# Moving the modulation's partial sums out of two feed-forward up projections

## The chip, the cores and the metric

One core of one Trainium2 chip runs the whole program. The metric is the device time of that core in microseconds (us); lower is better. Engines are named as the profile names them: PE is TensorE (PEld its weight loads), DVE is VectorE, ACT is ScalarE, POOL is GpSimd, SP is SyncE, which here only issues DMAs.

## What is computed

A small transformer stack on one sequence of 256 tokens of width 1024, to which 16 meta tokens are prepended (L = 272) for the first two layers. All of it is float32.

```python
h = concat([meta, x])
h = h + fox_attention(h)              # w_in: 4096 columns (q, k, v, gate) and 16 forget logits
h = h + conv_ffn(h)                   # down(silu(conv3(x @ gate)) * (x @ up)), hidden width 2816
h = h + hgrn2_mixer(h)                # w_in: f, q, g, v
h = h + conv_ffn(h)
h = h[:, 16:]
mod = (silu(c) @ w_ada + b_ada).reshape(3, 3, 1024)    # 9216 numbers
def sublayer(h, i, fn, w):
    shift, scale, gate = mod[i]
    u = rms_norm(h) * (1 + scale) + shift
    return h + w * gate * rms_norm(fn(u))
h = sublayer(h, 0, swiglu)            # "glu1"
h = sublayer(h, 1, token_mixer)       # "mix_in", two attentions, "branch", "mix_out"
h = sublayer(h, 2, swiglu)            # "glu2"
```

The change is about `mod`. It depends on nothing but `c`, `w_ada` and `b_ada`, so it can be worked out at any time before the three sublayers that use it.

## The kernel before

**The stream of weights.** Each projection is cut into units: 256 output columns with all 1024 input rows (1 MB), or 128 output columns with 2816 input rows for the down projections (1.4 MB). Two units, s = 0 and s = 1, make a pair, and a pair is one iteration of a hardware loop. SP loads a unit into `raw[s]`. The float32 product is made of three products of rounded values, so ACT rounds the unit to `w_hi[s]` (line 421, once PE has finished the unit that was in that slot), DVE subtracts to get `w_lo[s]` (L958), and PE multiplies hi by hi, hi by lo and lo by hi (L1899). When PE has done a unit, DVE (or ACT) evacuates its PSUM banks. In `ffn0_up` and `ffn1_up` that evacuation is long: a scale (L1344), six operations of the 3-tap convolution (L1348, L1353), another scale (L1359), a product (L1363) and a subtraction (L1365).

**The chains.** `w_ada` is cut into 36 pairs of 256 columns. For each pair POOL loads two halves of 512 KB into `ada_raw[0]` and `ada_raw[1]` (L1820, `load_modulation`); it issues each half when DVE has finished with what was there. DVE forms a running sum with 8 operations in a row, 4 for each half (`ada_half`: L969 for the first, L978 for the others; below, "a chain"). PE then adds up the 128 partitions with two matmuls of one column against ones (`ada_sums`, L1870), which land in bank 5 of PSUM. The chains are spread over the projections: inside `gemm`, after the split of each unit, DVE works on half a chain. The table `ADA` says which iterations carry one: name: (first pair, first iteration, number of iterations). `sums` in the PE program says after which iterations PE adds a pair up, one iteration after DVE has made it:

```python
                pe.wait_ge(ada_mult, p * 2 + 4)
                for s in range(2):
                    T_.matmul(ps[:, 5, bass.ds(p * 2 + s, 1)], ada_sum[:, s * P:(s + 1) * P], ones[:, 0:1],
                              start=True, stop=True).then_inc(ada_done, 1)
```

PE executes in order, so a wait for `ada_mult` (a finished chain) holds up the matmuls that stand behind it.

**Order.** Everything is ordered by hand: each engine has its own program, and semaphores tie them (`hi_ready`, `lo_ready`, `unit_done`, `banks_free`). The finished columns of `mod` are read from PSUM by `read_modulation`, from places named by `before_last` (between the last two iterations of a loop), and before bank 5 is needed for something else: `near_scores` waits for `mod_read`. Between the first and the second segment of `hgrn_in` (f, then q), DVE computes `f_all` from the gates with eight operations (L1388) and `kk` with one (L1390). POOL, when it has issued its ninth pair, clears `near` and `s_t` for the HGRN mixer with two MEMSETs (L1835, L1836).

Of the kernel before, what the change touches and what calls it, by code (L numbers as in the profile page):

```python
# [27 lines left out]
P = 128  # L28
# [96 lines left out]
def build_program(nc, t):  # L125
# [43 lines left out]
    ADA = {"fox_out": (0, 0, 1), "ffn0_up": (1, 4, 3), "ffn0_down": (4, 0, 3), "hgrn_in": (7, 0, 2), "hgrn_out": (9, 0, 1),  # L169
           "ffn1_up": (10, 5, 2), "ffn1_down": (12, 0, 3), "glu1_up": (15, 0, 11), "glu1_down": (26, 0, 2), "mix_in": (28, 0, 4), "glu2_up": (32, 0, 4)}  # L170
# [5 lines left out]
    with ctx:  # L176
# [230 lines left out]
        def _(act):  # L407
# [174 lines left out]
            nc.scalar.activation(c_silu, vecs("c_2", 0, KD), ACT.Sigmoid).then_inc(c_gate, 1)  # L582
# [363 lines left out]
        def _(dve):  # L946
# [37 lines left out]
            def gemm(name, evac=None, k=None, per=0, late=False, defer=False, ada=None, before_last=None):  # L984
                g = GEMMS[name]
                first, ada_it, ada_pairs = ADA[ada] if ada else (0, 0, 0)
                for i, (at, s) in enumerate(g["segs"]):
# [4 lines left out]
                    peel = before_last is not None or last and (defer or at + 2 * pairs >= N_UNITS or UNIT_SIZE[at + 2 * pairs] != g["size"])  # L992
# [178 lines left out]
            gemm("fox_in", copy_out(lambda it, s: proj1[:, bass.ds(it * 4 + 2 * s, 2), :], L), k=0)  # L1171
# [25 lines left out]
            dve.wait_ge(vec_ready, 4)  # L1197
            for i in range(2):
# [113 lines left out]
            dve.wait_ge(c_ready, 1)  # L1312
# [15 lines left out]
            def h_and_squares(it, s, pair):  # L1328

                h_of_down(it, s, pair)  # L1330
                if s > 0 and not (s == 2 and type(it) is int and it == KD // 2 - 1):
                    add_square("ffn1_down", it, s - 1)

            def conv_ffn(l):
# [35 lines left out]
                gemm(f"ffn{l}_up", evac, per=2, late=True, ada=f"ffn{l}_up", before_last=modulation_post0 if l else None)  # L1370
# [13 lines left out]
            gemm("hgrn_in", out_from(0), k=0, late=True, ada="hgrn_in")  # L1384
# [6 lines left out]
            def modulation_0():  # L1391
                read_modulation(1, 0, 18)
                pre_gain(0)
                dve.wait_ge(mod_set, 1)
                V.memset(lam_tmp[:, 0:1], 0.0).then_inc(mod_ready, 1)

            gemm("hgrn_in", out_from(8), k=1, before_last=modulation_0)
# [119 lines left out]
            def gained_tile(i, name):  # L1517

                def evac(it, s, pair):
                    if s < 2:  # L1520
# [3 lines left out]
                        V.tensor_scalar(y_raw[:, k, :], ps[:, 2 * s:2 * s + 1, 0:SEQ], mod_g[:, i, k], None, ALU.mult).then_inc(banks_free[s], 1)  # L1524
                    if s > 0 and not (s == 2 and type(it) is int and it == KD // 2 - 1):
# [64 lines left out]
            def modulation_1():  # L1590
                read_modulation(3, 24, 56)
                pre_gain(1)
                post_gain(1)
                dve.wait_ge(mod_set, 4)
                V.memset(lam_tmp[:, 0:1], 0.0).then_inc(mod_ready, 1)

            def modulation_2():
# [6 lines left out]
                dve.wait_ge(mod_set, 5)  # L1604
                V.memset(lam_tmp[:, 0:1], 0.0).then_inc(mod_ready, 1)

            def modulation_3():
                read_modulation(5, 64, 72)
                post_gain(2)
                dve.wait_ge(mod_set, 6)  # L1610

            def glu1():
# [13 lines left out]
                gemm("glu1_down", gained_tile(0, "glu1_down"), defer=True, ada="glu1_down", before_last=modulation_1)  # L1626
# [35 lines left out]
            gemm("mix_in", copy_out(lambda it, s: proj2[:, bass.ds(it * 4 + 2 * s, 2), :], SEQ), k=0, ada="mix_in", before_last=modulation_2)  # L1662
# [799 lines left out]
```

## Time and profile before

| | |
|---|---|
| median of 3 runs | 1517.8 us (1512.83 to 1521.1) |
| the profiled execution | 1515.93 us, its span 1514.3 us |
| PE busy | 1410.7 us, 93% of the span |
| DVE busy | 993.5 us, 66% |
| ACT busy | 600.9 us, 40% |
| POOL busy | 81.4 us, 5% |
| mean granted TensorE clock | 0.970 |

The span is the time from the first to the last instruction; the execution's own time is 1.6 us more. A busy share is an average over stages; the rows below are read by stage.

### The profile page before, as it was taken

Reading aid. Unit: us, or ns where it says so; the run is one execution under the profiler, and the core shown is the slowest. Engines: PE = TensorE matmul, PEld = TensorE weight load, DVE = VectorE, ACT = ScalarE, POOL = GpSimd, SP = SyncE. Lnnn points to the kernel's source line nnn. Section 1 sums busy time; section 2 is a strip of 40 time slices with the busy share of each in tenths; the row PEclk is TensorE's granted clock in tenths of the full one; section 3 lists DMA queues with packets and bytes.
Section 4 is the critical chain, followed back from the end, with each engine's and each line's share of the span. In section 5 each row is a group of like instructions: output and inputs, shape, how many; then the busy total and the mean of one; then the engine's idle time right before and its main releaser. Section 6 shows DMA issues by size and latency. Waiting matters only on the chain.

```text
span 1514.3 us, 29508 instructions
## 1 busy us (share of the span) xinstructions
PE 1410.7 (93%) x11888; PEld 1362.1 (90%) x11888; DVE 993.5 (66%) x1288; ACT 600.9 (40%) x590; POOL 81.4 (5%) x108
## 2 busy tenths in 40 slices
PE   5989898998999989899899899999899988899997
PEld 4988788998999989799899899999798878899997
DVE  4474455688765785568886687875685345796654
ACT  2344123443424424444343444343333454544432
POOL 2020000000000100000000011100020000000000
PEclk9999888999999999999999999999899999999998
DMA  5443204456775543345677577896373333475672
GB/s 167 139 116 107 84 1 140 153 182 218 201 219 179 165 132 101 127 163 185 204 203 218 163 250 259 271 267 201 111 259 125 112 123 107 146 243 187 187 191 66
DMA packets 263069, 252.53 MB, mean 167 GB/s; under 512 B 4681, under 2 KB 250572, under 8 KB 262996
## 3 DMA queue, kind: packets, MB, share of 16 engines
q1 hardware_dynamic: 251808, 212.37, 45.7%
q0 software_dynamic: 10992, 39.06, 7.6%
q8 instruction: 55, 0.90, 0.2%
q14 instruction: 18, 0.15, 0.0%
q10 hardware_dynamic: 196, 0.06, 0.0%
HBM read 250.42 MB, written 1.05 MB: 166 GB/s over the span
## 4 chain that ended last, share of the span: by engine, by line
PE 76%; DVE 11%; ACT 6%; issue 5%; DMA 1%; DVEq 0%; ACTq 0%; SPq 0%
PE ps L1899 62%; ACT w_hi L421 4%; DVE w_lo L958 3%; PE ps L1975 2%; PE ps L1923 2%; DVE proj L978 1%; PE ps L2124 1%; DMA raw<-in_fox_w_in 1%; PE ps L2059 1%; PE ps L2341 1%; PE ps L2109 1%; PE ps L2103 1%; DMA raw<-in_ffn_w_down 1%; DVE proj L1353 0%; PE ps L2020 0%
## 5 line engine op out<-in xcount | busy, mean ns | idle before, releaser
L1899 PE MATMUL ps<-x_hi,w_hi 128*128 128x272 f32 (+2 forms) x2208 | 642.3, 291 | 26.1 <-DVE w_lo L958 12.1
L1899 PE MATMUL ps<-x_lo,w_hi 128*128 128x272 f32 (+2 forms) x2208 | 633.2, 287 | 0.0
L1899 PE MATMUL ps<-x_hi,w_lo 128*128 128x272 f32 (+2 forms) x2208 | 632.9, 287 | 0.0
L958 DVE TENSOR_TENSOR w_lo<-raw,w_hi 128x2048 fp32r<-128x2048 f32 (+1 forms) x185 | 451.2, 2439 | 190.5 <-ACT w_hi L421 190.1
L421 ACT ACTIVATE w_hi<-raw 128x2048 fp32r<-128x2048 f32 (+1 forms) x185 | 374.3, 2023 | 409.4 <-PE ps L1899 376.3
L1899 PEld LDWEIGHTS ps<-x_hi,w_hi 128*128 128x128 f32 x2208 | 421.4, 191 | 33.4 <-issue 27.5
L1899 PEld LDWEIGHTS ps<-x_lo,w_hi 128*128 128x128 f32 x2208 | 421.7, 191 | 0.3
L1899 PEld LDWEIGHTS ps<-x_hi,w_lo 128*128 128x128 f32 x2208 | 421.8, 191 | 0.0
L1899 PE MATMUL ps<-g_hi,w_hi 128*128 128x256 f32 (+2 forms) x768 | 219.2, 285 | 8.6 <-DVE w_lo L958 3.3
L1899 PE MATMUL ps<-g_hi,w_lo 128*128 128x256 f32 (+2 forms) x768 | 217.8, 284 | 0.0
L1899 PE MATMUL ps<-g_lo,w_hi 128*128 128x256 f32 (+2 forms) x768 | 217.2, 283 | 0.0
L1899 PEld LDWEIGHTS ps<-g_hi,w_hi 128*128 128x128 f32 x768 | 145.4, 189 | 10.5 <-issue 3.5
L1899 PEld LDWEIGHTS ps<-g_lo,w_hi 128*128 128x128 f32 x768 | 145.8, 190 | 0.0
L1899 PEld LDWEIGHTS ps<-g_hi,w_lo 128*128 128x128 f32 x768 | 145.3, 189 | 0.0
L978 DVE SCALAR_TENSOR_TENSOR proj<-v_tok,small,proj 128x256 f32<-128x256 f32 x252 | 122.2, 485 | 7.7
L1820 POOL DMA_DIRECT2D v_tok<-in_w_ada x72 | 54.0, 751 | 1155.9 <-DVE proj L978 816.6
L1899 PE MATMUL ps<-proj_r,w_hi 128*128 128x258 f32 (+1 forms) x256 | 49.6, 296 | 7.8 <-DVE proj_r L1710 5.3
L1899 PEld LDWEIGHTS ps<-proj_r,w_hi 128*128 128x128 f32 x256 | 41.8, 199 | 8.8 <-issue 5.7
L481 ACT ACTIVATE proj<-ps 128x256 f32 (+2 forms) x20 | 8.5, 427 | 97.0 <-PE ps L1899 97.0
L1353 DVE SCALAR_TENSOR_TENSOR proj<-proj,cols 128x272 f32<-128x272 f32 (+1 forms) x88 | 39.6, 491 | 6.3 <-DVE proj L1348 3.4
L630 ACT ACTIVATE g_hi<-proj 128x544 f32 (+3 forms) x22 | 14.2, 648 | 70.5 <-DVE proj L1363 70.5
L1038 DVE COPY proj<-ps 128x544 f32 (+2 forms) x24 | 16.9, 702 | 36.2 <-PE ps L1899 31.5
(315 smaller groups left out, 1323.2 us busy)
## 6 DMA issues: line engine op xcount, KB each, us to landing
raw<-in_ffn_w_gate SPq DMA_DIRECT2D x44, 1024.0 KB, 5.3
raw<-in_ffn_w_up SPq DMA_DIRECT2D x44, 1024.0 KB, 5.3
raw<-in_ffn_w_down SPq DMA_DIRECT2D x32, 1408.0 KB, 7.0
v_tok<-in_w_ada POOLq DMA_DIRECT2D x72, 512.0 KB, 4.4
raw<-in_w_in SPq DMA_DIRECT2D x20, 1024.0 KB, 5.3
raw<-in_fox_w_in SPq DMA_DIRECT2D x16, 1024.0 KB, 5.8
raw<-in_hgrn_w_in SPq DMA_DIRECT2D x16, 1024.0 KB, 5.4
raw<-in_fox_w_out SPq DMA_DIRECT2D x4, 1024.0 KB, 4.8
```

What stands on the lines that cost most here:

```text
L421: nc.scalar.activation(w_hi[s][:, 0:size], raw[s][:, 0:size], ACT.Copy).then_inc(hi_ready, 1)
L958: V.tensor_tensor(w_lo[s][:, 0:size], raw[s][:, 0:size], w_hi[s][:, 0:size].bitcast(F32), ALU.subtract).then_inc(lo_ready, 1)
L978: ins = V.scalar_tensor_tensor(out=ada_sum if whole else ada_acc, in0=ada_raw[s][:, k, :], scalar=c_k, in1=ada_acc, op0=ALU.mult, op1=ALU.add)
L1038: V.tensor_copy(dst(it, s), ps[:, 2 * s:2 * s + 2, 0:T]).then_inc(banks_free[s], 1)
L1353: ins = V.scalar_tensor_tensor(out=conv[:, m, 0:T], in0=pad_a[:, m, w:w + T], scalar=col(w, it, m), in1=conv[:, m, 0:T], op0=ALU.mult, op1 ...
L1820: pool.dma_start(ada_raw[s], ada_w[:, KD // 2 * s:KD // 2 * (s + 1), bass.ds((it + first) * (2 * P), 2 * P)]).then_inc(ada_landed[s], 16)
L1899: ins = T_.matmul(dst, w[:, kt, m * P:(m + 1) * P], x[:, kt, 0:T], start=(kt == 0 and i == 0), stop=(kt == kts - 1 and i == 2))
L1923: ins = T_.matmul(ps[:, 2 * s + m, 0:T], wt[:, kt, m * P:(m + 1) * P], x[:, kt, 0:T], start=(kt == 0 and i == 0), stop=(kt == KD - 1 and i ...
L1975: ins = T_.matmul(ps[:, 4, 0:T], ones, sq[:, k, 0:T], start=(k == 0), stop=(k == KD - 1))
L2059: ins = T_.matmul(ps[:, b + 2 * e + bank, at:at + nk], proj1_flat[r, j * L + qt * P:j * L + (qt + 1) * P], proj1[r, 8 + j, 0:nk], start=Fa ...
L2103: T_.matmul(dst, c_diag[:, key0:key0 + P], shift_r[:, t0:L], start=(kt == 0), stop=False, skip_group_check=True)
L2109: ins = T_.matmul(ps[:, 2 * p + e, at:at + n], proj1_flat[r, (8 + j) * L + kt * P:(8 + j) * L + (kt + 1) * P], proj1[r, j, t0:L], start=Fa ...
```

## The change

The 36 chains are dealt out anew. `ffn0_up` loses 3 and `ffn1_up` loses 2. The first segment of `fox_in` gets 2, the q segment of `hgrn_in` gets 1 (`hgrn_q`), `glu1_down` goes from 2 to 3 and `mix_in` from 4 to 5. Nothing changes in how many there are, nor in what one consists of. With that go:

- The sums stand in columns 288 and up of bank 5 (`ADA_COL`), beside the forget logits, and the first four are copied out at once.
- silu(c) is made at the start: Exp on ACT, then an addition, a reciprocal and a product on DVE, instead of Sigmoid on ACT and a product on POOL.
- In the down projections PE adds a pair up after the first unit of the iteration instead of after the second (`sums_after=0`).
- `modulation_0`, `modulation_1` and `modulation_2` and the post gain of sublayer 0 are read inside the evacuation of a last iteration, instead of between two iterations; for this the last iteration is written out (`unroll_last`).
- POOL issues pairs 0 and 1 during `fox_in`, before it builds `c_diag`.

```diff
-    ADA = {"fox_out": (0, 0, 1), "ffn0_up": (1, 4, 3), "ffn0_down": (4, 0, 3), "hgrn_in": (7, 0, 2), "hgrn_out": (9, 0, 1),
-           "ffn1_up": (10, 5, 2), "ffn1_down": (12, 0, 3), "glu1_up": (15, 0, 11), "glu1_down": (26, 0, 2), "mix_in": (28, 0, 4), "glu2_up": (32, 0, 4)}
+    ADA = {"fox_in": (0, 1, 2), "fox_out": (2, 0, 1), "ffn0_down": (3, 0, 3), "hgrn_f": (6, 0, 2), "hgrn_q": (8, 0, 1), "hgrn_out": (9, 0, 1),
+           "ffn1_down": (10, 0, 3), "glu1_up": (13, 0, 11), "glu1_down": (24, 0, 3), "mix_in": (27, 0, 5), "glu2_up": (32, 0, 4)}
+    ADA_COL = 288
...
+            act.wait_ge(vec_ready, 1)
+            nc.scalar.activation(c_silu, vecs("c_2", 0, KD), ACT.Exp, scale=-1.0).then_inc(c_gate, 1)
...
-            nc.scalar.activation(c_silu, vecs("c_2", 0, KD), ACT.Sigmoid).then_inc(c_gate, 1)
...
             def modulation_post0():
-                read_modulation(2, 18, 24)
+                read_modulation(3, 18, 26)
...
-            gemm("fox_in", copy_out(lambda it, s: proj1[:, bass.ds(it * 4 + 2 * s, 2), :], L), k=0)
+            dve.wait_ge(c_gate, 1)
+            steps.done(V.tensor_scalar(c_silu, c_silu, 1.0, None, ALU.add))
+            steps.wait()
+            steps.done(V.reciprocal(c_silu, c_silu))
+            steps.wait()
+            V.tensor_tensor(c_silu, c_silu, vecs("c_2", 0, KD), ALU.mult).then_inc(c_ready, 1)
+            dve.wait_ge(c_ready, 1)
+            gemm("fox_in", copy_out(lambda it, s: proj1[:, bass.ds(it * 4 + 2 * s, 2), :], L), k=0, ada="fox_in")
+            dve.wait_ge(ada_done, 4 + 2)
+            V.tensor_copy(mod[:, 0:4], ps[:, 5, ADA_COL:ADA_COL + 4]).then_inc(mod_read, 1)
...
+                if type(it) is int and it == KD // 2 - 1 and s == 0:
+                    modulation_post0()
...
-                gemm(f"ffn{l}_up", evac, per=2, late=True, ada=f"ffn{l}_up", before_last=modulation_post0 if l else None)
+                gemm(f"ffn{l}_up", evac, per=2, late=True)
...
-            gemm("hgrn_in", out_from(8), k=1, before_last=modulation_0)
+            gemm("hgrn_in", q_out, k=1, ada="hgrn_q", unroll_last=True)
...
+            pool.wait_ge(unit_done, 2 + 1)
+            load_modulation(0, 2)
...
-            load_modulation(0, ADA["hgrn_out"][0])
+            load_modulation(2, ADA["hgrn_out"][0] - 2)
...
-                        if add:
-                            ada_sums(it + ada_before)
+                            if add and s == sums_after:
+                                ada_sums(it + ada_before)
...
-            gemm("ffn0_up", from_norm(1), xh, xl, L, late=lambda: norm_sum(1, L), ada="ffn0_up", sums=(5, 8))
-            gemm("ffn0_down", from_hidden(0), gh, gl, L, ada="ffn0_down", sums=(1, 4))
+            gemm("ffn0_up", from_norm(1), xh, xl, L, late=lambda: norm_sum(1, L))
+            gemm("ffn0_down", from_hidden(0), gh, gl, L, ada="ffn0_down", sums=(1, 4), sums_after=0)
...
-            gemm("hgrn_in", from_norm(2), xh, xl, L, k=1, ada="hgrn_out", sums=(0, 1))
+            gemm("hgrn_in", from_norm(2), xh, xl, L, k=1, ada="hgrn_q", sums=(0, 2))
...
-            gemm("ffn1_down", from_hidden(1), gh, gl, L - UNUSED, ada="ffn1_down", sums=(1, 4))
+            gemm("ffn1_down", from_hidden(1), gh, gl, L - UNUSED, ada="ffn1_down", sums=(1, 4), sums_after=0)
```

Three places in the order of instructions. The names: `w_lo<-raw,w_hi` is the split of a unit; `proj<-v_tok,small,proj` and `proj<-v_tok,small` are operations of a chain (`ada_raw` lies in `v_tok`); `proj<-ps,rstd` is an evacuation. Lines of the changed kernel are its own, a few more than those of the kernel before.

DVE, the loop of the iterations of `ffn0_up` that carry a chain, before:

```order
L958 TENSOR_TENSOR w_lo<-raw,w_hi 128x2048
L964 ISA
L965 ISA
L969 TENSOR_SCALAR proj<-v_tok,small 128x256
L122 ISA
L978 SCALAR_TENSOR_TENSOR proj<-v_tok,small,proj 128x256
...
L1348 TENSOR_SCALAR proj<-proj,cols 128x272
```

and in the changed kernel, the one loop that is left:

```order
L960 TENSOR_TENSOR w_lo<-raw,w_hi 128x2048
L1360 REGISTER_ALU
L1362 ISA
L1362 REGISTER_ALU
L1362 TENSOR_SCALAR proj<-proj,cols 128x272
```

The half chain between the split and the convolution is gone, and so is the other half behind the second split.

DVE, from the end of the f segment of `hgrn_in` into the q segment, before:

```order
L1390 TENSOR_SCALAR proj<-scratch 128x2176
L1013 UNCONDITIONAL_BRANCH
L1150 TENSOR_TENSOR proj<-ps,rstd 128x544
L958 TENSOR_TENSOR w_lo<-raw,w_hi 128x2048
L1150 TENSOR_TENSOR proj<-ps,rstd 128x544
L958 TENSOR_TENSOR w_lo<-raw,w_hi 128x2048
L1013 REGISTER_ALU
```

and now:

```order
L1404 TENSOR_SCALAR proj<-scratch 128x2176
L1015 UNCONDITIONAL_BRANCH
L1152 TENSOR_TENSOR proj<-ps,rstd 128x544
L960 TENSOR_TENSOR w_lo<-raw,w_hi 128x2048
L971 TENSOR_SCALAR proj<-v_tok,small 128x256
L980 SCALAR_TENSOR_TENSOR proj<-v_tok,small,proj 128x256 x3
L1152 TENSOR_TENSOR proj<-ps,rstd 128x544
L960 TENSOR_TENSOR w_lo<-raw,w_hi 128x2048
L980 SCALAR_TENSOR_TENSOR proj<-v_tok,small,proj 128x256 x4
L1015 REGISTER_ALU
```

The q segment's first iteration has a chain now; the eight operations of `f_all` and the one of `kk` ahead of it stand where they stood.

PE, the sum in the loop of `ffn1_down`, before (the last matmuls of the second unit, the sum, the branch back):

```order
L1899 MATMUL ps<-g_hi,w_lo 128x258
L1868 ISA
L1870 ISA
L1870 MATMUL ps<-const_f_sb,proj 128x1
L1870 ISA
L1870 MATMUL ps<-const_f_sb,proj 128x1
L1954 REGISTER_ALU
L1954 COMPARE_AND_BRANCH
```

and now (the last matmul of the first unit, the sum, the first matmul of the second unit):

```order
L1926 MATMUL ps<-g_hi,w_lo 128x258
L1895 ISA
L1897 ISA
L1897 MATMUL ps<-const_f_sb,proj 128x1
L1897 ISA
L1897 MATMUL ps<-const_f_sb,proj 128x1
L1915 REGISTER_ALU
L1926 MATMUL ps<-g_hi,w_hi 128x258
```

The sum stands one unit earlier on PE; the chain that it waits for stands where it stood on DVE.

## Rows read from the trace of the kernel before

**Rows 1.** The page: busy us (share of the span) xinstructions.

```profile
PE 1410.7 (93%) x11888; PEld 1362.1 (90%) x11888; DVE 993.5 (66%) x1288; ACT 600.9 (40%) x590; POOL 81.4 (5%) x108
```

**Rows 2.** Windows, ffn0_up: us, busy PE PEld DVE ACT POOL, clock, DMA, GB/s.

```profile
283.40:319.70 36.30, 36.30 (x290) 36.30 (x289) 28.93 (x37) 15.12 (x12) 0.00 (x0) 1.00 0.53 173
334.70:349.70 15.00, 13.02 (x102) 12.75 (x102) 13.18 (x20) 5.06 (x6) 1.52 (x3) 1.00 0.62 210
```

**Rows 3.** PE's waits, 320:400 (ffn0_up) and 717:786.3 (ffn1_up): total, times, longest.

```profile
PE ps L1899 <- DVE w_lo L958: 5.1, 5, 1.1
...
PE ps L1899 <- DVE w_lo L958: 4.2, 4, 1.4
```

**Rows 4.** The chain that ended last (start, us, what): a sum on PE.

```profile
1133.93 0.34 PE ps L1870 x4
```

**Rows 5.** Timeline of PE in ffn1_down: start, us, what, [idle before <-releaser].

```profile
819.94 0.36 PE L1899 MATMUL ps<-g_hi,w_hi 128*128 128x258 f32 x1 [0.28 <-DVE w_lo L958]
...
828.12 0.39 PE L1899 MATMUL ps<-g_hi,w_hi 128*128 128x258 f32 x1
...
836.15 0.50 PE L1870 MATMUL ps<-const_f_sb,proj 128*128 128x1 f32 x4
```

**Rows 6.** Timeline of DVE, ffn1_down: first and third of three second half chains.

```profile
810.66 2.04 DVE L978 SCALAR_TENSOR_TENSOR proj<-v_tok,small,proj 128x256 f32<-128x256 f32 x4
...
845.28 2.04 DVE L978 SCALAR_TENSOR_TENSOR proj<-v_tok,small,proj 128x256 f32<-128x256 f32 x4
```

**Rows 7.** Timelines, glu1_down: a second half chain on DVE, ACT behind the next unit.

```profile
1015.55 2.04 DVE L978 SCALAR_TENSOR_TENSOR proj<-v_tok,small,proj 128x256 f32<-128x256 f32 x4
1017.89 0.39 ACT L481 ACTIVATE proj<-ps 128x256 f32 x1 [5.38 <-PE ps L1899]
```

**Rows 8.** Timeline of DVE, ffn0_down: the evacuation behind a second half chain.

```profile
431.45 0.44 DVE L1067 TENSOR_TENSOR h<-h,ps 128x272 f32 x1 [0.78 <-PE ps L1899]
```

**Rows 9.** Timelines of DVE and PE, fox_in's first segment and its end.

```profile
60.45 0.73 DVE L1038 COPY proj<-ps 128x544 f32 x1 [1.93 <-PE ps L1899]
...
90.09 0.57 PE L1899 MATMUL ps<-x_hi,w_hi 128*128 128x272 f32 x1 [5.37 <-DVE scratch L1176]
```

**Rows 10.** Timeline of POOL, around the MEMSETs for the HGRN mixer.

```profile
497.99 0.75 POOL L1820 DMA_DIRECT2D v_tok<-in_w_ada  x1 [8.02 <-DVE proj L978]
498.73 0.65 POOL L1835 MEMSET scratch<- 128x640 f32 x1
499.30 3.01 POOL L1836 MEMSET scratch<- 128x3456 f32 x1
```

**Rows 11.** Timeline of DVE (last row PE): a first operation in ffn0_up, then hgrn_in.

```profile
323.88 0.34 DVE L969 TENSOR_SCALAR proj<-v_tok,small 128x256 f32<-128x256 f32 x1
...
495.31 2.04 DVE L978 SCALAR_TENSOR_TENSOR proj<-v_tok,small,proj 128x256 f32<-128x256 f32 x4
...
501.36 1.09 DVE L969 TENSOR_SCALAR proj<-v_tok,small 128x256 f32<-128x256 f32 x1
...
507.42 2.04 DVE L978 SCALAR_TENSOR_TENSOR proj<-v_tok,small,proj 128x256 f32<-128x256 f32 x4
509.37 2.73 DVE L1388 TENSOR_SCALAR scratch<-proj,small 128x272 f32<-128x272 f32 x8
512.14 1.30 DVE L1390 TENSOR_SCALAR proj<-scratch 128x2176 f32<-128x2176 f32 x1
...
517.70 2.29 DVE L958 TENSOR_TENSOR w_lo<-raw,w_hi 128x2048 fp32r<-128x2048 f32 x1 [0.80 <-ACT w_hi L421]
516.32 0.39 PE L1899 MATMUL ps<-x_hi,w_hi 128*128 128x272 f32 x1 [0.27 <-DVE w_lo L958]
```

**Rows 12.** An idle stretch of PE, and two windows (clock: third from last).

```profile
259.81 0.36 PE L1899 MATMUL ps<-x_hi,w_hi 128*128 128x272 f32 x1 [1.73 <-DVE x_lo L1135]
260.40:263.30 2.90, 2.90 (x14) 2.90 (x14) 2.02 (x6) 2.90 (x4) 0.00 (x0) 0.50 0.06 20
...
736.80:742.60 5.80, 5.80 (x48) 5.65 (x48) 5.42 (x11) 0.75 (x2) 0.75 (x1) 1.00 0.79 270
```

More of the change, by code:

```diff
@@ L982, in ada_half, with gemm @@
                 ins.then_inc(ada_mult, 1)
-            def gemm(name, evac=None, k=None, per=0, late=False, defer=False, ada=None, before_last=None):
+            def gemm(name, evac=None, k=None, per=0, late=False, defer=False, ada=None, before_last=None, unroll_last=False):
                 g = GEMMS[name]
@@ L991, in gemm @@
                     last = at + 2 * pairs == g["first"] + g["units"]
-                    peel = before_last is not None or last and (defer or at + 2 * pairs >= N_UNITS or UNIT_SIZE[at + 2 * pairs] != g["size"])
+                    peel = unroll_last or before_last is not None or last and (defer or at + 2 * pairs >= N_UNITS or UNIT_SIZE[at + 2 * pairs] != g["size"])
                     def body(it, size, ahead=False, defer=False, ada=False):
@@ L1382, in out_from @@
                 return normed_out(lambda it, s: proj1[:, bass.ds(it * 4 + (tile0 + 2 * s), 2), :])
-            gemm("hgrn_in", out_from(0), k=0, late=True, ada="hgrn_in")
+            gemm("hgrn_in", out_from(0), k=0, late=True, ada="hgrn_f")
             dve.wait_ge(gates_done, 4)
@@ L1390, in _, with q_out @@
             V.tensor_scalar(kk, f_all, -1.0, 1.0, ALU.mult, ALU.add).then_inc(f_ready, 1)
[L1391 to L1395, printed above, removed]
-            gemm("hgrn_in", out_from(8), k=1, before_last=modulation_0)
+            q_normed = out_from(8)
+            def q_out(it, s, pair):
+                q_normed(it, s, pair)
+                if type(it) is int and it == 1 and s == 1:
+                    read_modulation(2, 4, 18)
+                    pre_gain(0)
+                    dve.wait_ge(mod_set, 2)
+                    V.memset(lam_tmp[:, 0:1], 0.0).then_inc(mod_ready, 1)
+            gemm("hgrn_in", q_out, k=1, ada="hgrn_q", unroll_last=True)
             g_pair, v_pair = (GEMMS["hgrn_in"]["segs"][i][0] // 2 for i in (2, 3))
@@ L1625, in glu1 @@
                 clear_sum("glu1_down")
-                gemm("glu1_down", gained_tile(0, "glu1_down"), defer=True, ada="glu1_down", before_last=modulation_1)
+                gemm("glu1_down", gained_tile(0, "glu1_down"), defer=True, ada="glu1_down")
             def glu2():
@@ L1661, in _, with qkv_out @@
             scale_shifted(6, 5, 1)
-            gemm("mix_in", copy_out(lambda it, s: proj2[:, bass.ds(it * 4 + 2 * s, 2), :], SEQ), k=0, ada="mix_in", before_last=modulation_2)
+            qkv_copy = copy_out(lambda it, s: proj2[:, bass.ds(it * 4 + 2 * s, 2), :], SEQ)
+            def qkv_out(it, s, pair):
+                qkv_copy(it, s, pair)
+                if type(it) is int and it == 5 and s == 1:
+                    modulation_2()
+            gemm("mix_in", qkv_out, k=0, ada="mix_in", unroll_last=True)
             gates = GEMMS["mix_in"]["segs"][1][0] // 2
@@ L2021, in head_sums @@
                 ins.then_inc(hq_ss, 1)
-            gemm("fox_in", from_norm(0), xh, xl, L, k=0, late=forget_logits)
+            gemm("fox_in", from_norm(0), xh, xl, L, k=0, late=forget_logits, ada="fox_in", sums=(2, 4))
             pe.wait_ge(more_landed, 16 * 5)
```

45 lines of the change are left out of this document (23 added, 22 removed).

## The prediction

> **What bounds the kernel now.** I read the page's busy times first. PE is busy 93% of the span and DVE 66% [rows 1]: PE is the bound on average, so an operation on DVE costs only where PE waits for it. Where that is, the windows tell. In `ffn0_up` without a chain, 36.3 us hold three iterations (12.1 us each) and DVE is busy 28.93 us of them, 9.6 us an iteration; with a chain an iteration takes 15.0 us, DVE is busy 13.2 us of it and PE 13.0 [rows 2]. So the chain, about 3.9 us of DVE, does not fit into the 12.1 us that PE needs, because the convolution is there too. What it costs is in the waits of PE for the split `w_lo`: 5.1 us in five pieces in `ffn0_up`, 4.2 us in four in `ffn1_up` [rows 3]. These are the stretches that the chains leave.
>
> **What is removed.** 5.1 + 4.2 = 9.3 us of waiting on PE. The five sums that stood there took PE 0.34 us each [rows 4], 1.7 us; but the same five sums now stand in `fox_in` (2), `hgrn_in` q, `glu1_down` and `mix_in`, where PE is the bound, so 1.7 us come back. That cancels.
>
> **fox_in, first segment.** Here DVE has only a copy and a split per unit: behind the split it idles 1.93 us until PE is done [rows 9]. A half chain takes 2.04 us [rows 11], so the copy comes 0.1 us late, and the split behind it waits for ACT anyway. I cost the chains at nothing; without that cover they would cost four times 0.1 us. The end of the segment is on the path: PE waits 5.37 us there for `f_neg` (L1176) [rows 9], and DVE now copies four columns of PSUM ahead of it. No row has that copy; it lies between nothing and the 0.39 us that an engine needs to read 256 columns [rows 7]. I take 0.2. POOL's loads of pairs 0 and 1, and the silu of eight columns, lie beside PE's first units.
>
> **hgrn_in, the chain itself.** In the q segment's first iteration DVE now has two half chains. In the trace of before, the split of its fourth unit starts at 517.70, after 0.80 us of waiting for ACT, and ends at 520.0; PE starts the third unit at 516.32 [rows 11] and needs the fourth some 6 us later, at 522.3 (half of the 12.1 us of an iteration). A half chain of 2.0 us ahead of it, less the 0.8 us of waiting, brings it to 521.2. Covered. The modulation's reading behind the last unit lies in DVE's wait for ACT. Nothing.
>
> **hgrn_in, POOL's MEMSETs.** This is the term I find largest. POOL issues the load of pair 8 when DVE is through with pair 7's halves. Before, that was in the first iteration of f: half chain ends at 497.35, load issued at 497.99, 0.64 us later, then MEMSETs of 0.65 and 3.01 us [rows 10, 11]. Now pairs 6 and 7 are made in f, so pair 8 is issued one iteration later: half chain ends at 509.46, load at 510.1, MEMSETs from 510.85 to 514.5. At that time DVE works on L1388 (eight operations) and L1390, 509.37 to 513.44, and PE already waits 0.27 us for the split behind them at 516.32 [rows 11]: DVE has no slack there. What happens when such an operation meets the MEMSET can be seen: L969 takes 0.34 us elsewhere, but 1.09 us at 501.36, and it ends at 502.45, 0.14 us after the MEMSET's end at 502.31 [rows 10, 11]. L1388 and L1390 are of the same kind (TENSOR_SCALAR, SBUF to SBUF). So they will stand until both MEMSETs are through: the bounds are 0, if POOL has to wait instead, and 3.7 us, the two MEMSETs. I take 3.6, nearer to the row that shows DVE waiting.
> The Trainium skill (SBUF — State Buffer, Who interferes with whom) has it that GpSimd shares one pair of ports with VectorE, that a copy or tensor_scalar in a two-port mode and a GpSimd operation exclude each other for a whole instruction, and that whichever is issued first wins. By that rule the price is 3.6 us if POOL gets in between two of DVE's eight operations, and nothing if it does not. The row of L969 agrees with the rule; no row shows POOL trying to enter a burst.
>
> A wait of PE near 4 us brings more. After the 1.73 us wait at 259.81 the granted clock is 0.50 for about 3.5 us, which is the lower level, 1.2 GHz; behind the longest wait of `ffn1_up`, 1.4 us, which ends at the start of the window 736.80:742.60, it stays at 1.00, 2.4 GHz [rows 3, 12]. So behind the new wait I expect some 3.5 us at half clock, a loss of 1.7 us. Together 5.3 us.
>
> **The sum one unit earlier.** PE now asks for a pair's sum behind the first unit of the next iteration of a down projection. In `ffn1_down` DVE runs late: its second half chain ends at 812.70 and, in the third iteration, at 847.32 ; the middle one lies halfway, at 830.0 [rows 6]. PE's units are 8.0 us long (828.12 to 836.15) [rows 5]. Counted back from 819.94, with the sum between, the first unit of the iteration ended near 811.3. The sum would wait 1.5 us for 812.8; the next unit starts at 813.1 instead of 811.3, and the one after it at 821.2 instead of 819.94. It ends at 829.2, waits 0.9 us for the middle chain, and so again for the third. Going on so, the last unit ends 2.2 us later than before. In `glu1_down` the half chain ends at 1017.59 and ACT sees the unit at 1017.89 [rows 7]; the unit will come 0.34 us earlier, since the sum no longer stands ahead of it. So PE stands about 0.3 us three times: 0.9 us, bounds 0 and 1.5. In `ffn0_down` DVE idles 0.78 us between half chain and unit [rows 8]: no wait, but the third sum, which lay in a wait at the stage's end, moves ahead: 0.3 us. Behind the PE instruction that waits stand all matmuls of the second unit; DVE's evacuation waits for these, but has slack, so nothing more follows. These stalls are under 1.7 us, so I let the clock stay.
>
> **mix_in.** POOL's constants come one iteration later, in an iteration that has a chain again, as before. The reading of the modulation lies in a wait for ACT. Nothing but the sum.
>
> **The sum.** Gain 9.3. Costs 0.2 + 5.3 + 2.2 + 0.9 + 0.3 = 8.9. Net 0.4 us faster: the profiled execution's own 1515.9 us (span 1514.3) would be 1515.5. The median shown is 1517.8, 1.9 us above it; on its scale 1517.4, and I say 1517. A measurement of this kernel can tell about 0.5%, 7.6 us, from no change.
>
> **Rivals.**
> 1. The MEMSETs cost nothing, because DVE's eight operations follow so closely that POOL waits. Then 5.7 us faster, 1512. For it: the load issued at 510.1 itself may be held back. Against it: the row of L969. Chance 0.3, against 0.5 for my forecast.
> 2. Neither the MEMSETs nor the earlier sums cost: DVE, freed in `ffn1_up`, also enters `ffn1_down` earlier, and the stalls there vanish (2.2 + 0.9 back). Then 8.8 us faster, 1509. Against it: DVE's lateness in `ffn1_down` is made anew in each iteration by ACT's square and rounding. Chance 0.13.
> 3. Slower: each of the six new stalls in `ffn1_down` and `glu1_down` puts the clock to half. Price 1.7 us each by rows 12, up to 10 us: 1527. It decides from the fifth stall on. It needs stalls of 1.7 us and more; mine are 1.5, 0.9, 0.9 and 0.3. Chance 0.07.
> The change not doing what it says (chains in `fox_in` stalling PE) would cost 0.4 us by the above and is no case of its own.
>
> **Numbers.** Range: from rival 2 at 1509 to 1521, which is my forecast with the upper bounds (0.4 for the copy, 1.5 for `glu1_down`, 3.7 for the MEMSETs, some 1 us) and half clock behind two of the stalls. Faster by over 0.5% is at 1510.2 or less: rival 2 and a part of rival 1, 0.2. Slower by over 0.5%: 0.08. Within: 0.72.
>
> **What would show it.** No wait of PE for `w_lo` in the middle of `ffn0_up` and `ffn1_up`, iterations of 12.1 us in the first. L1388's eight operations spread over some 6 us, with MEMSETs of POOL inside, and PE's wait at the q segment's third unit near 4 us, then a granted clock of 0.50. Waits of PE for the chain's last operation in `ffn1_down`, 1.5, 0.9, 0.9 us. The forecast is wrong if L1388 and L1390 keep 2.73 and 1.30 us, or if the waits in the up projections turn out to have come from something else than the chain.

## The result, and the profile after

The changed kernel takes 1526.1 us (median of 8 runs, 1519.5 to 1531.7), the kernel before beside it 1514.7 us (8 runs, 1510.5 to 1521.1). The ratio is 1.0068, with a 95% interval of 1.0042 to 1.0095: 10 us slower, where the prediction had no change and a range up to 1521. The profiled execution was the longest of the eight, 1531.68 us with a span of 1530.0 us; a second one of the same program (the run called "again" below) had a span of 1527.4 us and a median of 1526.2 us. The text uses the first for rows, and the second where it says so.

The page of the changed kernel, busy times, beside [rows 1]:

```profile
PE 1422.2 (93%) x11888; PEld 1372.9 (90%) x11888; DVE 998.7 (65%) x1293; ACT 601.1 (39%) x590; POOL 81.2 (5%) x107
```

PE executes as many matmuls as before and is busy 11.5 us longer. In the trace of before a matmul of 272 columns takes 0.43 us where the granted clock is 0.50 (90 to 96 us) and 0.29 us where it is 1.00 (97 to 99 us). The mean granted clock fell from 0.970 to 0.962. So idle time is only a part of the loss, and time at half clock the other.

PE's matmuls are the same in the same order (but for the sums of the chains), so a stage can be compared by the starts of its first and of the next stage's first matmul in both traces. In us:

| stage | before | changed | again | what is there |
|---|---|---|---|---|
| fox_in, first segment | 60.7 | 61.0 | 61.1 | two chains |
| fox_in, k segment | 48.5 | 52.7 | 52.7 | a wait of 2.7 (below) |
| v segment and attention | 92.3 | 93.9 | 93.9 | clock |
| ffn0_up | 145.7 | 138.4 | 138.4 | three chains gone |
| ffn0_down | 69.4 | 69.8 | 69.9 | third sum |
| hgrn_in, from the end of f through q | 18.7 | 25.8 | 25.8 | the MEMSETs |
| hgrn_in g and v, with scores | 70.5 | 73.4 | 73.2 | a wait of 2.9 or 2.6 |
| rest of the mixer, then hgrn_out | 49.1 | 51.9 | 53.1 | clock |
| ffn1_up | 137.1 | 131.8 | 131.7 | two chains gone |
| ffn1_down and the turn to glu1 | 87.7 | 90.7 | 90.3 | three earlier sums |
| glu1_down and the turn to mix_in | 94.4 | 100.8 | 97.1 | earlier sums, a late load |

All other stages agree within 0.5 us, but for the start (0.2 to 0.8 us shorter). The two up projections gave back 12.7 us, more than was forecast. One profile is one execution, and some stages differ between executions of a like program by their time at half clock: `ffn1_up` took 129.6 to 131.8 us in the eleven profiles of the changed kernel and of the versions made from it, so its gain may be up to 2 us larger than the table has it. The loss is elsewhere, in five places.

**The up projections.** This window of the changed `ffn0_up` (columns as in [rows 2]) and the list of PE's waits there and in `ffn1_up`, which is empty where [rows 3] had nine, show the gain as forecast:

```profile
287.60:312.00 24.40, 24.40 (x196) 24.40 (x195) 19.44 (x25) 10.17 (x9) 0.00 (x0) 1.00 0.53 172
```

**The k segment of fox_in.** Timelines of DVE, POOL and PE, changed kernel:

```profile
92.80 0.55 DVE L1207 COPY cols<-ps 128x88 f32<-128x88 f32 x3
93.38 7.15 DVE L1210 TENSOR_TENSOR mod<-mod,cols 128x4 f32<-128x4 f32 x1
100.45 0.14 DVE L1212 TENSOR_SCALAR small<-cols 128x1 f32<-128x1 f32 x1
...
100.70 0.14 DVE L1214 TENSOR_SCALAR small<-cols 128x1 f32<-128x1 f32 x1
...
93.06 7.45 POOL L1857 TENSOR_TENSOR c_diag<-scratch,const_f_sb 128x4352 fp32r<-128x4352 f32 x1
...
100.94 0.47 PE L2047 MATMUL ps<-scratch,const_f_sb 128*128 128x272 f32 x1 [2.72 <-issue]
```

An addition of four columns takes 7.15 us: it lasts until POOL's operation is over, at 100.51 (93.06 + 7.45). Behind it stand L1212 to L1214, the last of which signals `small_done`; it ends at 100.84, and PE's head sums start at 100.94. The profile names no releaser, only "issue"; the order on DVE gives it. Behind the wait the clock is 0.50 from 101.8 to 105.0, which makes up the rest of the 4.2 us. In the kernel before, the operation that waits for POOL stands behind these small ones:

```profile
93.90 0.15 DVE L1199 TENSOR_SCALAR small<-cols 128x1 f32<-128x1 f32 x1
...
94.16 0.14 DVE L1201 TENSOR_SCALAR small<-cols 128x1 f32<-128x1 f32 x1
94.22 6.96 DVE L1204 TENSOR_TENSOR scratch<-scratch 1x128 f32<-1x128 f32 x1
```

So before, DVE lost the same 7 us, and nobody waited. The change put one small operation ahead of a signal. The line is in the change (it stands in the diff at add_behind below), but neither in the excerpt ahead of the prediction nor in the prediction: the working went by "a copy of four columns" and stopped there.

**hgrn_in, q.** DVE, POOL and PE, changed kernel, beside [rows 10, 11]:

```profile
507.85 6.52 DVE L1402 TENSOR_SCALAR scratch<-proj,small 128x272 f32<-128x272 f32 x8
514.40 1.29 DVE L1404 TENSOR_SCALAR proj<-scratch 128x2176 f32<-128x2176 f32 x1
...
509.31 0.65 POOL L1862 MEMSET scratch<- 128x640 f32 x1
509.88 3.01 POOL L1863 MEMSET scratch<- 128x3456 f32 x1
...
518.77 0.57 PE L1926 MATMUL ps<-x_hi,w_hi 128*128 128x272 f32 x1 [4.24 <-DVE w_lo L960]
```

and the window behind PE's wait:

```profile
518.20:525.00 6.80, 6.23 (x28) 6.26 (x29) 6.59 (x11) 1.39 (x2) 0.00 (x0) 0.50 0.57 170
```

The eight operations take 6.52 us instead of 2.73, and the MEMSETs lie inside them. PE waits 4.24 us, and the granted clock behind it is 0.50, the lower of its two levels, for 6.8 us. `w_lo` comes late because its split stands on DVE behind these operations.

**hgrn_in, g.** PE stops at 564.69 in the middle of a unit, with all its data there (timeline of the changed kernel):

```profile
567.57 0.59 PE L1926 MATMUL ps<-x_hi,w_lo 128*128 128x272 f32 x1 [2.88 <-issue]
```

Its DMA view of 564.90 to 565.40 (packets, MB, share) has one packet of instructions:

```profile
q8 instruction: 1, 0.02, 14.1%
```

It starts when PE has just stopped, and there is none in the 5 us ahead of it. That reads as PE waiting for its own program; the runs with a shifted program below test it. Behind it stand 6.6 us at half clock in this execution:

```profile
566.00:572.60 6.60, 5.03 (x22) 5.03 (x22) 3.35 (x7) 0.00 (x0) 0.00 (x0) 0.50 0.50 161
```

In the second profile the same wait, 2.61 us, had none behind it (the clock is 1.00 from 566 to 600), but another wait of 2.37 us followed at 572, so the stage came out as long.

**ffn1_down and glu1_down.** Timeline of PE, changed kernel (first three rows `ffn1_down`, the others `glu1_down`):

```profile
818.83 0.60 PE L1897 MATMUL ps<-const_f_sb,proj 128*128 128x1 f32 x4 [1.48 <-DVE proj L980]
836.39 0.60 PE L1897 MATMUL ps<-const_f_sb,proj 128*128 128x1 f32 x4 [1.00 <-DVE proj L980]
853.95 0.60 PE L1897 MATMUL ps<-const_f_sb,proj 128*128 128x1 f32 x4 [0.99 <-DVE proj L980]
...
1011.71 0.38 PE L1926 MATMUL ps<-g_hi,w_hi 128*128 128x256 f32 x1 [3.06 <-DVE g_lo L1641]
...
1029.92 0.28 PE L1926 MATMUL ps<-g_hi,w_lo 128*128 128x256 f32 x1
1030.64 0.60 PE L1897 MATMUL ps<-const_f_sb,proj 128*128 128x1 f32 x4 [0.43 <-DVE proj L980]
1031.10 0.37 PE L1926 MATMUL ps<-g_hi,w_hi 128*128 128x256 f32 x1
```

and the window over the first three:

```profile
818.00:856.00 38.00, 35.18 (x289) 34.79 (x290) 24.19 (x34) 12.96 (x10) 3.75 (x5) 1.00 0.76 223
```

The waits of 1.48, 1.00 and 0.99 us are there where the prediction had 1.5, 0.9, 0.9, and the clock over them stays at 1.00. The last three rows of the timeline tell what a sum costs PE: from the matmul ahead of it to the one behind it, 1.18 us, less the 0.43 of waiting and the 0.12 by which one such matmul follows another, is 0.63 us, and not the 0.34 that the prediction took from [rows 4]. The busy time of a sum is no measure of it: it reads 0.34 there, 0.50 in [rows 5] and 0.60 here. The 3.06 us for `g_lo` goes back to a load of `w_down` for which ACT waited 5.43 us, against 3.45 in the trace of before; in the second profile it is 1.15 us. So its length is not fixed by the program.

### The profile page after: what moved, and what is told of

Its sections match the earlier page's. It is cut to its first block, busy times and chain, and to the rows that moved or that the text cites. A ratio compares the mean times of both kernels' runs of the same rounds, so it can differ in the third digit from the quotient of the medians.

```text
span 1530.0 us, 29512 instructions
## 1 busy us (share of the span) xinstructions
PE 1422.2 (93%) x11888; PEld 1372.9 (90%) x11888; DVE 998.7 (65%) x1293; ACT 601.1 (39%) x590; POOL 81.2 (5%) x107
## 4 chain that ended last, share of the span: by engine, by line
PE 79%; DVE 9%; ACT 5%; issue 5%; DMA 2%; SPq 0%; ACTq 0%; DVEq 0%
PE ps L1926 66%; ACT w_hi L422 3%; DVE w_lo L960 2%; PE ps L2002 2%; PE ps L1950 2%; DVE proj L980 1%; PE ps L2151 1%; DMA raw<-in_fox_w_in 1%; PE ps L2086 1%; PE ps L1897 1%; PE ps L2368 1%; DMA raw<-in_ffn_w_down 1%; PE ps L2136 1%; PE ps L2130 1%; PE ps L2047 1%
## 5 line engine op out<-in xcount | busy, mean ns | idle before, releaser
L1926 PEld LDWEIGHTS ps<-x_hi,w_hi 128*128 128x128 f32 x2208 | 423.8, 192 | 27.9 <-issue 25.8
L1926 PEld LDWEIGHTS ps<-g_hi,w_hi 128*128 128x128 f32 x768 | 146.1, 190 | 10.8 <-DVE g_lo L1641 3.3
L980 DVE SCALAR_TENSOR_TENSOR proj<-v_tok,small,proj 128x256 f32<-128x256 f32 x252 | 122.1, 485 | 7.7
L482 ACT ACTIVATE proj<-ps 128x256 f32 (+2 forms) x20 | 8.5, 427 | 101.8 <-PE ps L1926 101.8
L1950 PE MATMUL ps<-x_hi,w_hi 128*128 128x256 f32 (+1 forms) x96 | 30.9, 322 | 9.7 <-DVE x_lo L1106 5.8
L1926 PE MATMUL ps<-proj_r,w_lo 128*128 128x258 f32 (+1 forms) x128 | 38.3, 299 | 0.0
```

Of the source, the lines that this page charges most:

```text
L980: ins = V.scalar_tensor_tensor(out=ada_sum if whole else ada_acc, in0=ada_raw[s][:, k, :], scalar=c_k, in1=ada_acc, op0=ALU.mult, op1=ALU.add)
L1926: ins = T_.matmul(dst, w[:, kt, m * P:(m + 1) * P], x[:, kt, 0:T], start=(kt == 0 and i == 0), stop=(kt == kts - 1 and i == 2))
L1950: ins = T_.matmul(ps[:, 2 * s + m, 0:T], wt[:, kt, m * P:(m + 1) * P], x[:, kt, 0:T], start=(kt == 0 and i == 0), stop=(kt == KD - 1 and i ...
```

## The experiments

Each is given with its ratio to the kernel before, run beside it, and the 95% interval; 0.001 is 1.5 us. Medians of the kernel before differ by up to 4 us from one group of runs to the next, so ratios are compared, not medians. Each version has one profile, so a stage's time is of one execution.

**again**: the changed kernel once more, no edit.

> The changed kernel once more. If the four new idle stretches of PE are made by the program's order (2.7 us ahead of the head sums in the k segment of fox_in, 4.2 us for w_lo in q of hgrn_in, 2.9 us inside a unit of the g segment, 3.1 us for g_lo in glu1_down), each is there again within 0.3 us. If one is made by how transfers happened to fall, it has another length: I expect that of the 3.1 us, where ACT waited for a load that landed some 2 us later than in the kernel before, and not of the others. The profiled execution then takes 1524 to 1532 us.

1.0062 (1.0041 to 1.0084), profiled span 1527.4 us. The first three waits were 2.67, 4.25 and 2.61 us, as expected, and the one for `g_lo` 1.15: only that one did not recur at its length. A second wait without releaser, 2.37 us, came in this execution at 572.

**add_behind**: the addition behind `small_done`.

```diff
-            dve.wait_ge(mod_read, 1)
-            V.tensor_tensor(mod[:, 0:4], mod[:, 0:4], cols[:, 3, 0:4], ALU.add).then_inc(mod_set, 1)
             for i in range(2):
...
             V.tensor_scalar(subln, vec("da_subln_2"), 1.0 - LAMBDA_INIT, None, ALU.mult).then_inc(small_done, 1)
+            dve.wait_ge(mod_read, 1)
+            V.tensor_tensor(mod[:, 0:4], mod[:, 0:4], cols[:, 3, 0:4], ALU.add).then_inc(mod_set, 1)
```

> The addition of b_ada to the first four sums (L1210) stands behind the operation that signals small_done, instead of ahead of the gains. Theory (DVE's addition waits out POOL's 7.45 us operation, and small_done, which stands behind it, is what PE's head sums wait for): the gains end before 95 us, the addition itself takes some 7 us, PE's 2.7 us wait ahead of the head sums is gone, and with it part of the half clock behind: 3 to 5 us faster than the changed kernel. Rival (the 2.7 us are a wait for PE's instructions, since the profile names no releaser): the wait stays at 2.7 us and nothing is gained.

1.0032 (1.0014 to 1.0050), 0.30% or 4.5 us below "again" (for this and the other differences of two ratios the intervals allow some 4 to 5 us either way); the k segment took 48.0 us instead of 52.7. DVE and PE in that kernel:

```profile
93.06 0.14 DVE L1212 TENSOR_SCALAR small<-cols 128x1 f32<-128x1 f32 x1
93.13 6.83 DVE L1214 TENSOR_TENSOR mod<-mod,cols 128x4 f32<-128x4 f32 x1
...
97.38 2.00 PE L2047 MATMUL ps<-scratch,const_f_sb 128*128 128x272 f32 x8
```

The addition still takes 6.83 us and holds nobody up; PE's wait is gone. The first theory holds, and the rival, that this too was a wait for instructions, falls.

**add_scalar**: the addition at its place, with another kind of operation.

```diff
-            V.tensor_tensor(mod[:, 0:4], mod[:, 0:4], cols[:, 3, 0:4], ALU.add).then_inc(mod_set, 1)
+            for k in range(4):
+                ins = V.tensor_scalar(mod[:, k:k + 1], mod[:, k:k + 1], cols[:, 3, k:k + 1], None, ALU.add)
+            ins.then_inc(mod_set, 1)
```

> The changed kernel with the addition at its place, but as four TENSOR_SCALAR operations of one column each instead of one TENSOR_TENSOR. In the kernel before, TENSOR_SCALAR operations of one column took 0.14 us beside POOL's 7.4 us operation (L1199, 93.90 to 94.30), while the TENSOR_TENSOR behind them took 6.96 us. Theory (it is the kind of operation that waits for POOL): the four take 0.14 us each, small_done is signalled by 95 us, and PE's 2.7 us wait is gone, as in add_behind. Rival (any operation of DVE that comes first behind the copies is held): the first of the four takes 7 us, and PE waits 2.7 us.

1.0024 (0.9999 to 1.0048), the k segment 48.3 us. DVE there:

```profile
95.09 0.57 DVE L1211 TENSOR_SCALAR mod<-mod,cols 128x1 f32<-128x1 f32 x4
95.58 0.14 DVE L1214 TENSOR_SCALAR small<-cols 128x1 f32<-128x1 f32 x1
...
95.82 0.14 DVE L1216 TENSOR_SCALAR small<-cols 128x1 f32<-128x1 f32 x1
95.89 6.47 DVE L1219 TENSOR_TENSOR scratch<-scratch 1x128 f32<-1x128 f32 x1
```

Four additions in 0.57 us beside POOL's operation, and the next operation with two inputs from SBUF takes 6.47 us. Among operations this small it is the kind that waits. The Trainium skill (SBUF — State Buffer, Who interferes with whom) says so: a DVE instruction with two SBUF inputs contends with a GpSimd instruction that reads SBUF. These rows agree. TENSOR_SCALAR as such is not free of it: the eight of 128x272 above took 6.52 us beside POOL's MEMSETs.

**zero_early**: POOL's MEMSETs where they stood in time before the change.

```diff
-            load_modulation(2, ADA["hgrn_out"][0] - 2)
+            load_modulation(2, ADA["hgrn_q"][0] - 2)
             pool.wait_ge(unit_done, GEMMS["hgrn_in"]["first"] + 2 + 2)
             G.memset(near, 0.0)
             G.memset(s_t, 0.0).then_inc(mixer_zero, 1)
+            load_modulation(ADA["hgrn_q"][0], 1)
```

> POOL's two MEMSETs stand ahead of the load of pair 8 again, one iteration earlier. Theory (MEMSETs hold DVE's L1402 and L1404): these two take 2.7 and 1.3 us again, PE's wait for w_lo in q falls from 4.2 to about 0.3 us and no half clock follows: 5 to 7 us faster than the changed kernel. Rival (the half clock comes anyway at the next idle stretch): 4 us faster.

1.0007 (0.9989 to 1.0024), 0.55% or 8.3 us below "again". The stage from the end of f through q took 19.4 us instead of 25.8:

```profile
508.98 2.88 DVE L1402 TENSOR_SCALAR scratch<-proj,small 128x272 f32<-128x272 f32 x8
...
516.27 0.36 PE L1927 MATMUL ps<-x_hi,w_hi 128*128 128x272 f32 x1 [0.61 <-DVE w_lo L960]
...
510.00:530.00 20.00, 19.39 (x156) 19.34 (x155) 16.40 (x25) 8.28 (x7) 0.11 (x1) 1.00 0.59 191
```

DVE's eight operations are back at 2.88 us, PE's wait at 0.61, and the clock stays at 1.00. 6.4 us in the stage, 5 to 7 expected.

**sums_late**: sums after the second unit in the three down projections.

```diff
-            gemm("ffn1_down", from_hidden(1), gh, gl, L - UNUSED, ada="ffn1_down", sums=(1, 4), sums_after=0)
+            gemm("ffn1_down", from_hidden(1), gh, gl, L - UNUSED, ada="ffn1_down", sums=(1, 4))
...
-                if type(it) is int and it == KD // 2 - 1 and s == 0:
+                if type(it) is int and it == KD // 2 - 1 and s == 2:
                     modulation_post0()
```

(The same two edits for `glu1_down` and `modulation_1`, and the first for `ffn0_down`.)

> PE adds up a pair after the second unit again in ffn0_down, ffn1_down and glu1_down; the modulation is read at the end of the last iteration. Theory (six stalls of PE behind first units): the waits of 1.5, 1.0, 1.0 us in ffn1_down and three of 0.4 in glu1_down are gone, 3.5 to 5 us faster than the changed kernel. Rival (DVE is late by its own chain, and what PE does not wait for the chain it then waits for w_lo): the waits come back as waits for w_lo, and less than 2 us are gained.

1.0004 (0.9988 to 1.0021), 0.58% or 8.8 us below "again". The waits for `proj L980` are gone from the list of PE's waits in `ffn1_down`. What is left there:

```profile
PE ps L1926 <- DVE w_lo L960: 0.9, 2, 0.6
PE ps L1926 <- DVE g_lo L1379: 0.6, 1, 0.6
```

The changed kernel's own list has, beside the second of these lines,

```profile
PE ps L1897 <- DVE proj L980: 3.5, 3, 1.5
```

Of the 3.5 us, 0.9 came back as waits for `w_lo`, as the rival had it, but not more. The three stages took 0.5, 3.0 and 1.6 us less, 5.0 together (rounded) as expected. But the last of these holds the turn to `mix_in`, which took 25.2 to 28.9 us in the fourteen profiles with its time at half clock. The units of `glu1_down` alone took 66.5 us before, 69.1 in "again" and 66.6 here, so the earlier sums cost 2.5 us there and not 1.6. The units of `ffn1_down` alone took 68.0, 71.0 and 68.0. That makes 6.0 us from the three stages, 1 us above what was expected. The whole gained more still; see below.

**three**: the three edits together.

> The three edits of add_behind, zero_early and sums_late together. Theory (the three costs are separate waits of PE, each with the half clock behind it): the medians' differences add up, 7.4 + 8.8 + 9.5 below the changed kernel's 1526.2, so about 1501, and at least 1507 if what each gained beyond its own wait and clock (about 4.7, 6.4 and 5.0 us in its own stage) was shared. Rival (one disturbance, which any of the three edits ends): no better than the best of them, 1515 to 1518.

0.9944 (0.9918 to 0.9969), median 1510.7 against 1517.2: faster than the kernel before, by 8.5 us by the ratio. Against "again" that is 1.18%, 17.9 us, with some 5 us either way. The three alone sum to 21.6 us by the ratios and to 16.1 us by what their own stages lost (4.7, 6.4, 5.0). Both lie within it. The theory's times, 1501 to 1507 us, were too low: they were on the scale of the earlier group, whose kernel before had a median 2.3 us lower, and 1510.7 is 1508.4 on it. The rival of one common disturbance falls: together they are 0.6% better than the best of them.

**three_pad, three_pad64, three_pad192, after_pad192, before_pad128**: the same programs, with PE's instructions moved in memory.

```diff
             pe.sem_inc(unit_done, 2)
+            for _ in range(128):
+                pe.wait_ge(unit_done, 2)
             pe.sem_inc(ada_done, 2)
```

> As three, with 128 waits that are already satisfied at the start of PE's program, while PE idles for its first data, so that everything behind stands 128 instructions later in memory. Theory (the 2.3 to 2.9 us that PE idles in the middle of a unit of the g segment, with no releaser, are a wait for its own instructions: a 16 KB instruction transfer starts there at 565.0): the wait moves to another place or becomes shorter, as it did against the kernel before, and the program is up to 4 us faster or slower. Rival (something else in that unit): 2.3 to 2.9 us in the same unit.

> As three, with PE's program 64 instructions later in memory. Theory (PE's idle stretches without a releaser in 530 to 580 are waits for its instructions, and where they fall hangs on where a 16 KB piece of the program ends): their sum is another than the 2.9 us of three and the 5.8 us of the version with 128, between 2.5 and 6 us, at other matmuls. Rival: the same places as in three.

> As three_pad64, with 192 instructions. By the theory this stands 64 instructions ahead of the place of the program in three, counted round a piece of 256, with waits of 2.5 to 6 us at yet other matmuls; the four versions are within 3 us of each other, since each piece is waited for somewhere in the dense part. Rival: one of the four has no such wait and is 3 us or more faster than three.

> The changed kernel with PE's program 192 instructions later in memory, which left three with one wait of 1.3 us for instructions where there had been 2.9. Theory (the place of the program in memory is one part of the loss, apart from the three waits): the 2.6 to 2.9 us inside the unit of the g segment is gone, the stage from g to the last scores takes about 70.1 us instead of 73.2, and the median is 2 to 4 us below the changed kernel's 1526. Rival (the shift helps only together with the three edits, since the waits ahead decide when PE comes to the dense part): less than 1 us.

> The kernel before, with PE's program 128 instructions later in memory. In the kernel before PE waits 1.15 and 1.61 us without a releaser in the dense part. Theory (every version has such waits, by the place of the program, between 1.3 and 5.8 us in all): other places, the same sum within 3 us, the median within 3 us of the kernel before either way. Rival (before had the best place by luck and any shift costs): 2.5 to 4 us slower.

| | ratio (95%) | waits without releaser, 530 to 580, us | g and v stage, us |
|---|---|---|---|
| before | 1 | 1.15 + 1.61 | 70.5 |
| after, again | 1.0068, 1.0062 | 2.88; 2.61 + 2.37 | 73.4; 73.2 |
| three | 0.9944 (0.9918 to 0.9969) | 2.88 | 73.1 |
| three_pad64 | 0.9925 (0.9900 to 0.9950) | 1.46 + 3.20 | 73.5 |
| three_pad (128) | 0.9947 (0.9922 to 0.9971) | 1.77 + 0.76 + 3.30 | 73.9 |
| three_pad192 | 0.9916 (0.9884 to 0.9948) | 1.34 | 70.1 |
| after_pad192 | 1.0034 (1.0010 to 1.0057) | 1.35 + 0.82 | 70.5 |
| before_pad128 | 0.9995 (0.9972 to 1.0018) | 1.27 | 70.6 |

The longest such wait of before, of three_pad and of three_pad192, on PE:

```profile
540.54 0.66 PE L2161 MATMUL ps<-proj 128*32 128x32 f32 x49 [1.61 <-issue]
```

```profile
563.11 0.47 PE L2191 MATMUL ps<-proj 128*32 128x32 f32 x29 [3.30 <-issue]
```

```profile
536.36 0.44 PE L2191 MATMUL ps<-proj 128*32 128x32 f32 x27 [1.34 <-issue]
```

The waits move with the place of the program, as the theory has it, and an edit that computes nothing changes this stage between 70.1 and 73.9 us. For the changed kernel the shift gains 2.7 us in the stage itself: this part of the loss is apart from the three others. In the whole it gains 0.28%, 4.2 us, but with some 5 us either way that is not told from nothing, nor are the ratios of the four versions of three told from each other. One expectation fell: the versions of three do not all wait alike, and one has no wait above 1.34 us, as the rival to three_pad192 said. The rival to before_pad128 fell too: the kernel before was not lucky alone, since its shifted version is as fast. That what PE waits for is its instructions is inferred from the shift and from the packets of instructions; no row names it. Before had 2.8 us of such waits and still took 70.5 us. They fell between scores (L2161), where PE waits for DVE too, and not inside a unit; that this is the reason was not tried.

**chains_out**: the kernel before without the five chains of the up projections. It leaves out five of the 36 pairs of `w_ada`.

```diff
-    ADA = {"fox_out": (0, 0, 1), "ffn0_up": (1, 4, 3), "ffn0_down": (4, 0, 3), "hgrn_in": (7, 0, 2), "hgrn_out": (9, 0, 1),
-           "ffn1_up": (10, 5, 2), "ffn1_down": (12, 0, 3), ...
+    ADA = {"fox_out": (0, 0, 1), "ffn0_down": (1, 0, 3), "hgrn_in": (4, 0, 2), "hgrn_out": (6, 0, 1),
+           "ffn1_down": (7, 0, 3), ...
```

> The kernel before, with the five chains of ffn0_up and ffn1_up not made at all (31 pairs of w_ada are loaded and summed instead of 36, so ten columns of the modulation hold nothing); everything else stands where it stood. It measures the gain alone. The prediction's terms: waits of 9.3 us and five sums of 0.34 us, 1.7 us, together 11.0 us below the kernel before. Rival (the two stages were 7.3 and 5.4 us shorter in the changed kernel, so that a sum costs PE 0.7 us and not 0.34): 12.7 us. Rival on the other side (what a freed DVE gives there is lost again at the next stage): under 8 us.

0.9929 (0.9906 to 0.9952): 10.8 us faster than before, with an interval of 7.3 to 14.3. It can't tell 11.0 from 12.7, but excludes most of "under 8". `ffn0_up` took 138.4 us, as in the changed kernel. The gain is real and is kept in the whole.

## Why the prediction was wrong, step by step

**What bounds the kernel, and the gain: right.** 9.3 us of waits, and with five sums at the 0.63 us measured, not 0.34, 12.5; the stages gave 12.7, though that they agree so well is partly luck, since `ffn1_up` varies by 2 us. The step on the sums still cancels, because each stands elsewhere now.

**fox_in, first segment: right in the chains** (the stage took 0.3 us more, where the forecast's copy and two sums made 0.9; the wait at its end became 5.05 us). **Its end: this is the step that failed.** The prediction followed the copy of four columns and not what is done with them: the addition of `b_ada`, which the change puts ahead of the signal `small_done`, and which waits out POOL's 7.45 us. Shown by add_behind and add_scalar: 4.2 to 4.7 us in its stage, for a term of 0.2; it is the largest single miss. The row that would have told it, 6.96 us for an operation of one row that takes 0.27 in the changed kernel once POOL is done, stood in the trace of before.

**The MEMSETs: right in mechanism, place and wait** (3.8 us more on L1402, wait 4.24 us); rival 1 fell. **The clock behind it was mis-sized**: 3.5 us at half clock expected, after the 1.73 us wait of [rows 12]; it was 6.8 in the two profiles of the changed kernel and in that of after_pad192, and 3.4 in those of add_behind, sums_late and add_scalar, which all have the same wait of 4.25 us. The stage lost 7.1 us with 6.8 us at half clock and 5.7 to 5.9 with 3.4, with one sum in it, where 5.3 and a sum of 0.34 were expected.

**The sum one unit earlier: right in ffn1_down** (1.48, 1.00, 0.99 for 1.5, 0.9, 0.9; 3.0 us for 2.2). In `glu1_down` 0.43, 0.42 and 0.42 for three times 0.3; by the two rows that the prediction names there, 1017.59 and 1017.89 less 0.34, the wait would have been 0.04, so that its 0.3 is not derived. The three waits and the third sum are 1.9 of the 2.5 us; the other 0.6 is open. `ffn0_down` 0.5 for 0.3. `mix_in` 0.5 for the one sum.

**Missing: the place of the program in memory.** 2.7 us in the g segment. No part of the prediction, nor a rival, had it.

**Rival 3, the slower side**, had half clock behind the stalls of the down projections. That is wrong: the clock is 1.00 in the window 818:856 and, in `glu1_down`, from 1026 to 1066. It had the right direction by another mechanism, and its 1527 us is near the measured time by luck. Rival 2 fell with the waits in `ffn1_down`.

The terms together, from stages: gain 12.7; costs 0.3 (fox_in) + 4.2 (k) + 7.1 (q) + 2.7 (g) + 3.0 (`ffn1_down`) + 2.5 (`glu1_down`) + 0.5 (`ffn0_down`) + 0.5 (`mix_in`) = 20.8. That makes 8.1 us slower, of the 9.4 to 10.3 that the ratios 1.0062 and 1.0068 give, inside both intervals (from 6.2 us). The rest is not settled. The traces show where it can lie: the attention, the rest of the HGRN mixer and `hgrn_out`, whose program is unchanged, took 1.6 us and 2.8 to 4.0 us more, with the granted clock lower there in these executions. Before and before_pad128 were at half clock for 90 and 87 us of the span, the changed kernel for 118 and 111. But the profile of after_pad192, slower than before, has 90, and that of chains_out, the kernel before with less work, has 112. That clock differs between executions of like programs (the second of these stages took 49 to 53 us in the fourteen profiles, and the attention 91 to 98), so whether the change causes it or two profiles happened to have it is open. The same holds for the 2 to 3 us that zero_early and sums_late gained beyond their stages; the intervals allow them to be nothing.

## What to carry to other kernels

An operation that is added to an engine's program costs less by its own length than by what it is stuck behind and who stands behind it: read the added line's kind (two inputs from SBUF), what POOL does at that time, and the next signal. Put signals that others wait for ahead of work that can be held up, and follow every value that a change copies to the place where it is used. When work is dealt out anew, the moves of waits pay or cost more than the work: with the MEMSETs in their old place, the sums behind the second unit, the addition behind the signal and PE's program shifted by 192 instructions, the same redistribution runs at 0.9916 (0.9884 to 0.9948) of the kernel before, 1507.2 us against 1518.6, the lowest ratio here, though not told from those of three and three_pad64.

## What was not expected of the hardware

- PE stood still for up to 3.3 us with no releaser among small matmuls written out one behind the other (three_pad, 563), or in the unit behind them (2.88 us, changed kernel, 567). With 64, 128 or 192 satisfied waits at the start of its program the stops moved, and with 192 their sum fell to 1.3 us (three_pad192). The best reading is a wait for its own instructions; the profile shows it only as "issue" and as a packet of instructions in the DMA view.
- Beside a POOL operation of 7.4 us that reads SBUF, DVE's one-column TENSOR_SCALAR takes 0.14 us and a TENSOR_TENSOR of 128x4, or of a single row, 7.15 and 6.96 us.
- Two MEMSETs of POOL, 0.65 and 3.01 us, got in between DVE's eight TENSOR_SCALARs of 128x272, which took 6.52 us instead of 2.73.
- Idle stretches of 1.5 us and less left the clock at 1.00 (818:856), one of 2.61 us did in one execution (again, 566:600); one of 4.24 us brought 3.4 us at half clock in some executions and 6.8 in others.
- A sum of two matmuls of one column costs PE 0.63 us between two full units, where its busy time reads from 0.34 to 0.60 us.
